# Decode attention moved out of the prompt's sixteen steps: 42 of its 128 steps go between the products of values and gate, the rest are spread over the prompt's heads

## The reference

```python
# layer 0: conv mixer, then x = x + o and the gated per-layer embedding
h = rms_norm(x, norm_g); a, b, z = split(h @ w_in, 3)
u = a * sigmoid(b); c = silu(layer_norm(depthwise_conv31(u_ext)))
o = (c * silu(z)) @ w_out
# shared keys, values and forget values, from x after layer 0
k = rms_norm(h @ kv_w[:, :1024]); v = h @ kv_w[:, 1024:2048]; logf = log_sigmoid(...)
# layer 1: forgetting attention, 16 heads of 64
q = rms_norm(h @ w_q[:, :1024]); z = h @ w_q[:, 1024:]
s = q k^T / 8 + c_q - c_k;  p = softmax(masked s);  o = p v        # c = cumsum(logf)
x = x + (o * silu(z)) @ w_out
# then the gated per-layer embedding again
```

## Time and profile before

| | |
|---|---|
| device time, median of 3 runs | 2547.67 us (2546.33 to 2551.48) |
| the profiled execution's own time | 2547.7 us |
| its span in the trace | 2546.0 us |
| TensorE busy | 2300.0 us, 90% |
| VectorE, ScalarE, GpSimd busy | 55%, 37%, 45% |
| mean granted TensorE clock | 0.958 of 2.4 GHz |
| DMA over the span | 456.25 MB, mean 179 GB/s |

### The profile page before, as it was taken

The page is one execution under the profiler, slowest core; times in us unless marked ns, Lnnn a source line. Parts: engine busy times, 40 slices in busy tenths (PEclk is TensorE's granted clock), DMA queues, the critical chain, the costliest instruction groups (busy, mean ns, idle before and its releaser), DMA issues.

```text
span 2546.0 us, 45948 instructions
## 1 busy us (share of the span) xinstructions
PE 2300.0 (90%) x15044; PEld 1862.7 (73%) x15044; DVE 1403.1 (55%) x1981; ACT 948.5 (37%) x1596; POOL 1134.8 (45%) x751
## 2 busy tenths in 40 slices
PE   5999999997458999989999996899999999899899
PEld 3999999997248998979989994445445455354499
DVE  4789988898791013166555663344443444444523
ACT  4555656665351012233102331434433344244311
POOL 0798889988563214434545544222222222220221
PEclk7999999998769999989999998999999999999999
DMA  2222222222033121025332427999999999999312
GB/s 110 71 74 68 72 80 64 72 75 70 19 107 130 45 68 42 27 92 159 121 126 103 175 94 273 383 405 383 380 397 371 341 381 381 367 372 391 147 51 81
DMA packets 142255, 456.25 MB, mean 179 GB/s; under 512 B 27441, under 2 KB 36274, under 8 KB 141170
## 3 DMA queue, kind: packets, MB, share of 16 engines
q1 hardware_dynamic: 119762, 387.73, 41.7%
q0 software_dynamic: 19712, 55.03, 6.3%
q10 hardware_dynamic: 2592, 11.14, 1.1%
HBM read 399.78 MB, written 56.13 MB: 179 GB/s over the span
## 4 chain that ended last, share of the span: by engine, by line
PE 59%; POOL 12%; issue 9%; DVE 9%; DMA 6%; ACT 4%; SPq 1%; ACTq 0%; POOLq 0%; DVEq 0%
PE PS L507 10%; PE PS L509 10%; PE PS L508 10%; POOL ACC L1239 6%; PE PS L808 4%; PE PS L787 4%; PE PS L758 4%; DMA KV<-ck 3%; PE PS L741 3%; PE PS L825 3%; PE PS L515 2%; PE PS L720 2%; POOL WL L1212 2%; DMA KV<-cv 1%; POOL ACC L1235 1%
## 5 line engine op out<-in xcount | busy, mean ns | idle before, releaser
L1212 POOL TENSOR_TENSOR WL<-RAW,WH 128x1024 fp32r<-128x1024 f32 (+1 forms) x113 | 293.2, 2595 | 393.7 <-ACT WH L879 386.7
L1570 DVE SCALAR_TENSOR_TENSOR PS<-UX,CWT,PS 128x1024 f32<-128x1024 f32 (+1 forms) x672 | 466.3, 782 | 0.0
L540 PE MATMUL PS<-HH,WH 128*128 128x384 f32 (+1 forms) x1152 | 378.5, 329 | 20.7 <-DVE HL L1556 20.7
L542 PE MATMUL PS<-HH,WL 128*128 128x384 f32 (+1 forms) x1152 | 377.4, 328 | 0.0
L541 PE MATMUL PS<-HL,WH 128*128 128x384 f32 (+1 forms) x1152 | 377.2, 327 | 0.0
L1358 POOL DMA_DIRECT2D QI<-qX_scr x128 | 76.7, 606 | 509.3 <-PE PS L720 505.7
L1239 POOL TENSOR_TENSOR ACC<-ACC,PROD 128x1088 f32<-128x1088 f32 x112 | 284.6, 2541 | 31.3 <-ACT PROD L931 25.1
L507 PE MATMUL PS<-GH,WH 128*128 128x384 f32 (+1 forms) x768 | 256.4, 334 | 16.7 <-DVE KC L1641 10.1
L509 PE MATMUL PS<-GH,WL 128*128 128x384 f32 (+1 forms) x768 | 255.4, 333 | 0.0
L508 PE MATMUL PS<-GL,WH 128*128 128x384 f32 (+1 forms) x768 | 254.2, 331 | 0.0
L540 PEld LDWEIGHTS PS<-HH,WH 128*128 128x128 f32 x1152 | 217.3, 189 | 24.7 <-issue 13.7
(11 more groups left out here) (229 smaller groups left out, 4625.3 us busy)
## 6 DMA issues: line engine op xcount, KB each, us to landing
KV<-ck SPq DMA_DIRECT2D x256, 512.0 KB, 10.5
KV<-cv SPq DMA_DIRECT2D x256, 512.0 KB, 10.8
RAW<-wA SPq DMA_DIRECT2D x48, 512.0 KB, 3.5
RAW<-wB SPq DMA_DIRECT2D x33, 512.0 KB, 3.5
QI<-qX_scr POOLq DMA_DIRECT2D x192, 64.0 KB, 5.5
RAW<-wP SPq DMA_DIRECT2D x16, 640.0 KB, 3.9
zT_scr<-ZS ACTq DMA_DIRECT2D x16, 544.0 KB, 2.7
Z<-zT_scr SPq DMA_DIRECT2D x16, 544.0 KB, 3.6
```

The lines of the kernel that those rows point to most:

```text
L540: pe.matmul(out, WH[w][:, kk], HH[:, k, a:b], start=k == 0, stop=False)
L542: mm = pe.matmul(out, WL[w][:, kk], HH[:, k, a:b], start=False, stop=k == KD - 1)
L1212: pool.tensor_tensor(WL[s][:, 0:n], RAW[s][:, 0:n], WH[s][:, 0:n].bitcast(F32), ALU.subtract).then_inc(s_lo, 1)
L1570: i = dve.scalar_tensor_tensor(out=o, in0=x, scalar=w[:, j:j + 1], in1=o, op0=ALU.mult, op1=ALU.add)
```

## The change

The decode attention gets its own step number g = 16 b + t and its own helpers (`decode_half`), and its 128 steps no longer go with the prompt's 128. A step is two halves (h = 2g and 2g + 1).

- The units come in the order forget values, keys, queries, values, gate. Steps 0 to 41 are put between the k-blocks of the last 14 of them: none in the first two value units, 2 in each of the other six, 3 in each of the first two gate units and 4 in each of the last six.
- Two steps (42, 43) come between the last unit and the first prompt step. The other 86 are spread evenly over prompt steps ("slots" x) 0 to 125: 86 of the slots have one and 42 have none.
- While the units run the pages have 2 buffers, after them 3 (before: 4, in attention only).
- On ScalarE a slot is now: copy of the decode scores, `Exp` of slot x, copy of the transposed probabilities of slot x-1, decode exponentials.
- The residual stream `X2` leaves to DRAM (`xS_scr`) after layer 0 and comes back as `X3` in attention; the first two page buffers lie where `X2` was. The past forget values are summed in the embedding phase, the new ones in the key and query units; V and gate of the prompt have two buffers each; the loops of attention are written out.
- GpSimd loads the weights of the value and gate units, since SP is then on the pages.

The core of the diff:

```diff
-U_CONV, U_OUT, U_PLE, U_K, U_V, U_F, U_Q, U_Z, U_TAIL = 0, 48, 64, 72, 80, 88, 89, 97, 105
+U_CONV, U_OUT, U_PLE, U_F, U_K, U_Q, U_V, U_Z, U_TAIL = 0, 48, 64, 72, 73, 81, 89, 97, 105
...
+        def unit_steps(u):
+
+            if u < U_V + 2:
+                return 0, 0
+            if u < U_Z:
+                return 2 * (u - U_V - 2), 2
+            m = u - U_Z
+            return (12 + 3 * m, 3) if m < 2 else (18 + 4 * (m - 2), 4)
+
+        SPOTS = {0: (), 2: (1, 3, 5, 7), 3: (1, 2, 3, 5, 6, 7), 4: tuple(range(8))}
...
+        def half_after(u, k):
+
+            g, n = unit_steps(u)
+            return 2 * g + SPOTS[n].index(k) if k in SPOTS[n] else None
...
+        G_UNITS, G_LEAD = 42, 2
+        N_SLOTS, N_STEPS = 16 * PAIRS, 16 * DB
+
+        def steps_by(x):
+
+            return min(N_STEPS + 2, G_UNITS + G_LEAD + (x + 1) * (N_STEPS + 2 - G_UNITS - G_LEAD) // (N_SLOTS - 2))
+
+        def step_of(x):
+
+            return steps_by(x - 1) if steps_by(x) > steps_by(x - 1) else None
...
+        def ring(g):
+            return g % 2 if g < G_UNITS else (g - G_UNITS) % 3
...
+            def pages(g):
+
+                b, t, s = g // 16, g % 16, ring(g)
...
+                    if kk == 0:
+                        if g == G_UNITS + 2:
+                            sp.wait_ge(s_vst, 32 * PAIRS)
+                            for x in range(2):
+                                sp.wait_ge(s_gst[x], 16 * PAIRS // 2)
+                        elif g >= G_UNITS + 3:
+                            sp.wait_ge(s_dd, g - 2)
+                        elif g >= 2:
+                            sp.wait_ge(s_dd, g - 1)
+                    sp.dma_start(KV[s][:, kk, :], at(ck if t < NG else cv, page)).then_inc(s_kv[s], 16)
...
+                if u == U_F + 2:
+                    sp.wait_ge(s_x2, KD)
+                    sp.dma_start(xS, X2[:]).then_inc(s_xs, 16)
...
+                if u == U_K + 7:
+                    sp.wait_ge(s_xs, 16)
+                    sp.wait_ge(s_gl, KD)
+                    pages(0)
+                if u == U_K + 9:
+                    pages(1)
...
+            for g in range(2, N_STEPS):
+                pages(g)
...
-                    first_unit()
+                        out = unit_bank(st, r)[:, 0:b - a]
+                        pe.matmul(out, WH[w][:, kk], GH[:, k, a:b], start=k == 0, stop=False)
+                        pe.matmul(out, WH[w][:, kk], GL[:, k, a:b], start=False, stop=False)
+                        mm = pe.matmul(out, WL[w][:, kk], GH[:, k, a:b], start=False, stop=k == KD - 1)
+                    if k == KD - 1:
+                        mm.then_inc(s_unit, 1)
+                    h = half_after(u, k)
+                    if h is not None:
+                        decode_half(h, 0)
...
+            def decode_half(h, ev):
+
+                b, t, second = h // 32, h // 2 % 16, h % 2
+                if not second:
+                    if t == 0 and b > 0:
+                        decode_pv(b - 1, NG - 1)
+                    elif b == DB:
+                        return
+                    elif 0 < t < NG:
+                        decode_scores(b, t)
+                    elif t == NG:
+                        new_transpose(b, ev)
+                    elif t > NG:
+                        decode_pv(b, t - NG - 1)
                 else:
-                    pe.wait_ge(s_kc, m)
-                    main(U_K + m, s)
-                    norm(m - 1)
-
-            def v_unit(m, s, i):
-                pe.wait_ge(s_kc, PAIRS + m)
-                main(U_V + m, s)
-                if isinstance(m, int) and m == 0:
-                    norm(PAIRS - 1)
+                    if t == 1 and b > 0:
+                        heads_transpose(b - 1, ev)
+                    elif b == DB:
+                        return
+                    elif t == 0:
+                        decode_scores(b, t)
+                    elif t == NG - 1:
+                        new_scores(b)
+                    elif t >= NG:
+                        decode_transpose(b, t - NG, ev)
...
-            pe.wait_ge(s_bcon, 1)
-            pe.wait_ge(s_pad2, 5)
-            pe.wait_ge(s_knw, 32)
-            pe.wait_ge(s_zc, PAIRS)
-            steps(pe, att_step)
+            for h in range(2 * G_UNITS, 2 * (G_UNITS + G_LEAD)):
+                decode_half(h, 0)
+            pe.wait_ge(s_zx, PAIRS)
+            h = 2 * (G_UNITS + G_LEAD) - 1
+            for x in range(N_SLOTS):
+                b, t, g = x // 16, x % 16, step_of(x)
+                scores(b, t)
+                if g is not None:
+                    h = 2 * g
+                    decode_half(h, evacs(x - 2))
+                if x > 0:
+                    prompt_transpose(x - 1, h)
+                if g is not None:
+                    h = 2 * g + 1
+                    decode_half(h, evacs(x - 1))
+                if t == 0 and b > 0:
+                    prompt_pv(b - 1, NQ - 1)
+                if b > 0:
+                    out_product(b, t)
+                if t >= 2 and t % 2 == 0:
+                    prompt_pv(b, t // 2 - 1)
+            prompt_transpose(N_SLOTS - 1, h)
+            prompt_pv(PAIRS - 1, NQ - 1)
...
-                    if started(b) or t > 0:
...
-                        atleast(act, s_pv, NQ * bb + tp // 2)
-                        for c in range((n + 511) // 512):
-                            a, e = 512 * c, min(n, 512 * c + 512)
-                            act.wait_ge(s_trp, evacs(bb, tp, c))
-                            act.activation(PT[tp % 2][:, a:e], PS[:, 5 + c, 0:e - a], ACT.Copy).then_inc(s_ev, 1)
-                    if not real:
-                        continue
-                    n = P * (item + 1)
-                    act.wait_ge(s_nm, 16 * b + t + 1)
-                    atleast(act, s_trp, evacs(b, t - 2) if started(b) or t > 1 else 0)
-                    act.activation(PP[hl][:, 0:n], PS[:, 2 * hl:2 * hl + 2, :].rearrange("p a n -> p (a n)")[:, 0:n],
...
-                    if t < NG:
...
-                        act.wait_ge(s_dd, 16 * b + t + 1)
-                        atleast(act, s_td, 9 * b)
-                        act.activation(SC[:, 512 * t:512 * t + 512], PS[:, 4, :], ACT.Copy).then_inc(s_sc, 1)
-                        continue
...
+            def scores_out(b, t):
...
+                act.wait_ge(s_dd, 16 * b + t + 1)
+                atleast(act, s_td, 9 * b)
+                act.activation(SC[:, 512 * t:512 * t + 512], PS[:, 4, :], ACT.Copy).then_inc(s_sc, 1)
...
+            def probs_out(b, t):
                 j = t - NG
                 act.wait_ge(s_td, 9 * b + j + 2)
...
                 act.activation(PTD[j % 2][:], PS[:, 6, :].rearrange("p (k n) -> p k n", n=P),
                                ACT.Copy).then_inc(s_dv, 1)
+                if j < NG - 1:
+                    dec_exp(j + 1)
...
+            silu(PAIRS - 1)
+
+
+            def prompt_exp(x):
+
+                hl = x % 2
+                n = P * (order[x % 16 // 2] + 1)
+                act.wait_ge(s_nm, x + 1)
+                atleast(act, s_trp, evacs(x - 2))
+                act.activation(PP[hl][:, 0:n], PS[:, 2 * hl:2 * hl + 2, :].rearrange("p a n -> p (a n)")[:, 0:n],
+                               ACT.Exp, bias=NMX[hl][:], accum_out=SMP[hl][:]).then_inc(s_p, 1)
+
+            def prompt_evac(x):
+
+                n = P * (order[x % 16 // 2] + 1)
+                atleast(act, s_pv, NQ * (x // 16) + x % 16 // 2)
+                for c in range((n + 511) // 512):
+                    a, e = 512 * c, min(n, 512 * c + 512)
+                    act.wait_ge(s_trp, evacs(x, c))
+                    act.activation(PT[x % 2][:, a:e], PS[:, 5 + c, 0:e - a], ACT.Copy).then_inc(s_ev, 1)
+
+            for h in range(2 * G_UNITS, 2 * (G_UNITS + G_LEAD)):
+                decode_half(h)
+            for x in range(N_SLOTS):
+                g = step_of(x)
+                if g is not None:
+                    decode_half(2 * g)
+                prompt_exp(x)
+                if x > 0:
+                    prompt_evac(x - 1)
+                if x == 3:
+                    act.wait_ge(s_unit, U_TAIL - U_OUT)
+                    act.dma_start(X3[:], xS).then_inc(s_xs, 16)
+                if g is not None:
+                    decode_half(2 * g + 1)
+            prompt_evac(N_SLOTS - 1)
```

1497 lines of the change are left out of this document (757 added, 740 removed).

## The result

The changed kernel takes 2758.12 us (median of 4 runs, 2751.49 to 2764.41) against 2549.57 us (2546.33 to 2555.20): a ratio of 1.082, 95% interval 1.079 to 1.085. It is slower, as forecast, but by 8.2% and not by 4.4%; the time lies 53 us above the range.

What follows compares the result with a forecast made beforehand. TensorE was taken to bound the kernel, with DMA just behind in attention. 2547.7 + 115 (units) - 25 (attention) + 25 (clock) = 2662.7, said as 2660 us; its own range 2610 to 2705, the overall range 2515 to 2705.

Steps and rivals of the forecast that it cites:

- gap ahead of attention: Between the last unit and the first attention slot: taken as 12 us, where the kernel before had 19.7 us.
- signs named for being wrong: Out products right behind transposes with pairs under 85 us; gate units over 27 us; first slot >20 us after last unit.
- those for being right: Gate units with four steps 22 to 25 us; last unit to attention's end 780 to 830 us; TensorE under 85% busy.
- The steps' work in the units: Units: 42 decode steps at a mean of 2.34 us lengthen TensorE's path by 98 us.
- Pages in the gate units: Six gate units with four steps: page transfers at 388 GB/s take 24.5 us against 21.6 of TensorE; +17 us.
- The upper bound: Units: +144 us if with two buffers a step waits for nearly a full landing, 8.0 us a step in 24 steps.
- the second rival: Gate units: two page buffers for 24 steps bind, a landing taking 10.5 us; whole 2689 us; chance 0.13.
- Waits in attention: Attention: TensorE waits 171 us for the copy to `PT` behind the `Exp`, plus 3 us draining after the last slot.
- Work in attention: Attention: TensorE's work of 722 us less 103 us for 44 steps moved out leaves 619 us.
- The clock: Attention: about 20 falls of TensorE's granted clock at 1.25 us each, +25 us; bounds 0 and 131 us.
- The rest, taken as nothing: Elsewhere: `X2` traffic, past sums, small copies and weight loads lie under other work; 0 us, some 5 without cover.
- TensorE stays full: Attention: VectorE and ScalarE keep ahead, waits near 5 us a pair, 679 us; whole 2512 us; chance 0.21.

Runs made afterwards that it cites:

- the run with added products: Changed kernel with ten unread small products ahead of the transposes and ten behind in each attention slot without a decode step; 2730.97 us, ratio 1.0725.
- ScalarE's order: Changed kernel with ScalarE's slot order put back: copy to `PT`, then `Exp`, then decode copies; 2660.36 us, ratio 1.045.
- both orders: Changed kernel with ScalarE's and TensorE's slot orders put back, transposes of the previous head ahead of both halves of the step; 2632.61 us, ratio 1.0335.
- the dense run with the changed kernel's orders: Changed kernel with attention's 86 steps one in each of the first 86 slots, none in the last 42; 2764.55 us, ratio 1.085.
- the counterpart with short waits: The spread run with attention's 86 steps one in each of the first 86 slots, none in the last 42; 2651.51 us, ratio 1.041.
- the spread run: Both orders, plus past forget values loaded after the embedding's input, and series and running sum split over two units each; 2624.86 us, ratio 1.030.
- TensorE's alone: Changed kernel with TensorE's slot order put back, ScalarE's `Exp` still ahead of the copy to `PT`; 2819.05 us, ratio 1.106.

## Why the prediction was right and wrong

Against the forecast sum of 2662.7 us the profiled execution is 101.7 us longer. The direction was right, and so was the chain behind the waits; the sizes of four terms were not, the clock's above all. By term: steps' work in the units -2, pages +27, gap ahead of attention +2, waits -16, work in attention +15, the clock +55, what was taken as nothing +22 and -2.

Of the signs named for being wrong one appeared (gate units over 27 us: four of the six with four steps took 29.4 to 31.2). Of those for being right two failed: gate units of 22 to 25 us, and 780 to 830 us from the last unit to the end of attention (886.7).

*The steps' work in the units, +98: right.* Two steps make a value unit 18.4 us where it was 13.85, so 2.28 us a step against 2.34. Without waits for pages the units are 568.0 us, 103.7 more than before, 7.6 of them in the two units that wait for VectorE, below; 96 are left.

*Pages in the gate units, +17: too small by 27 us.* Pages and the clock behind them cost 43.6 us (611.6 - 568.0). That the bytes of the pages bind was right; what was wrong is the rate. I put 388 GB/s, from attention's pairs; the gate units shown above ran at 306 to 333, and the fastest of the eight at 356. The upper bound was also added up wrong: at 8.0 us a step six units take 192 us, 62 more than their 130 us of work and not 46, so it should read +160 in place of +144, and the second rival 2705 in place of 2689. The measured +147 lies under that. With two buffers DMA is at times idle until one is free (share 0.85 to 0.98), while a page lands in 5.7 to 6.1 us (median), not in the 10.5 of the second rival. How much of the lower rate is due to that, and how much to the unit's own stores and loads beside the pages, was not taken apart.

*Waits in attention, 171 + 3: near, 158 us.* The chain was the right one, as the slot above and the runs on the orders show: the single wait is 2.7 us for 1024 keys. In pairs 1 to 7 TensorE idles 1.8 us in a slot without a step, as put, 1.0 us in one with a step of scores (put: 1.5) and 0.9 us in one with a step of values (put: 0.95).

*Work in attention, 619: 15 us too small.* At the full clock it is 634 us (next paragraph). The 722 us for the kernel before rest on two windows that stand some 4 us off the pairs' borders. By the first prompt scores of each pair, b=3 lasts from 1865.4 to 1971.2 us, 105.8 us with 94.4 busy, where I read 97.4 and 91.4; b=4 lasts 103.3 us, where I read 111.7. The eight pairs are busy for 750 us, 26 of them at the lower clock, so 737 at the full one; less 103 for the steps this is 634. Their idle time is 60 us, 7.5 and not 5.2 us a pair.

*The clock, +25: the step that failed, by 55 us.* "If one slot in four of the 77 without values falls, about 20 falls at 1.25 us": the number of falls was near (25 stretches at the lower clock in the attention), but they last 6.9 us on the mean and up to 17, not the length of one group of products. Together they are 172 us at 1.2 GHz, and TensorE is busy for 161 of them. At the full clock that work takes half, so the low clock costs 80 us, as the run with added products says too. This is inside the bounds of 0 and 131. I costed a fall by the longer group of products just behind the wait, and should have taken the whole stretch until the granted clock is back. Not all of it belongs to the waits for `PT`: 34 of the 172 us are in the first pair, whose clock is 0.83 here and still 0.85, 0.84 and 0.87 with ScalarE's order, both orders and the added products. Behind the first pair these runs have 0.99, 0.97 and 0.99, the changed kernel 0.91. What holds the clock down in the first pair was not tested. The Trainium skill, in "TensorE: Matmul & The Clock Gate", the section on HAM oscillation, tells of falls that come back in every round, behind waits for DMA; those waits are longer than any for `PT` here. That falls come back, the traces of the changed kernel (25 stretches) and of the last slots of the dense run with the changed kernel's orders (0.81 to 0.83) agree; the counterpart with short waits, at 0.95 to 1.00 there, hardly shows it.

*The rest, taken as nothing: +22 us, less 2 at the end.* The start of the units is 14.2 us later. ScalarE waits 8.77 us for the embedding's input; with that input loaded ahead of the past forget values, in the spread run, the units began 5.6 us earlier:

```profile
960.76 2.11 ACT L1119 ACTIVATE PH<-PR 128x1088 fp32r<-128x1088 f32 x2 [8.77 <-DMA PR<-pT]
```

And in a query unit VectorE's running sum stands ahead of the scaling that frees TensorE's banks:

```profile
1268.18 1.42 DVE L1814 TENSOR_TENSOR KC<-PS,RSTD 128x384 f32<-128x384 f32 x3 [2.22 <-PE PS L701]
...
1278.43 1.35 DVE L1826 SCALAR_TENSOR_TENSOR KN<-KC,CST,RS 128x1088 f32<-128x1088 f32 x1
1279.70 0.71 DVE L1876 TENSOR_SCALAR FL<-FL 16x1088 f32<-16x1088 f32 x1
1280.45 5.47 DVE L1879 TENSOR_TENSOR_SCAN FL<-FL,ZERO 16x1024 f32<-16x1024 f32 x9
1285.85 1.39 DVE L1814 TENSOR_TENSOR KC<-PS,RSTD 128x384 f32<-128x384 f32 x3
```

"Beside products of 12 us and more" was no cover: of a unit VectorE had 2.22 us left ahead of the scaling, and the sums take over 6 us. The other 8.6 us of the late start lie in the embedding phase, beside the past sums on VectorE (busy 87 us from 955 us to the units, 41 in the kernel before); their cause was not tested alone.

*The rivals.* "TensorE stays full" was to be decided by waits under 90 us. With both orders put back TensorE idles 81 us in attention, and the time is 2632.6, not 2512: the units still cost 141 us, and attention takes 745.6 us, not 679. Its waits are nearly twice the 45 us, its work is the 634 us, and the clock (0.95) costs some 32. "The pages bind" holds by its size, 44 us, though not by its landing time. So both the forecast and this rival happened, with a clock that was worse than in either.

## What to carry to other kernels

A step that is moved from one full stage of an engine into another costs its whole length there, and what it leaves behind may be not a shorter stage but a wait that it had covered, as here. Look, for each pair of instructions that share a buffer or bank, at what stands between them on both engines once the cover is gone, and put the short copy that is waited for ahead of the long operation that waits itself. Try the two engines' orders together and not one alone: ScalarE's alone gave 98 us here, TensorE's alone lost 61, both gave 126. Price waits on TensorE with the clock, by the whole stretch at the lower level: here the attention had 158 us of idle time and 80 us of slower products besides. Set the windows of a sum on the borders that the instructions show.

## What the runs showed of the hardware

- The changed kernel's attention and the dense run's pair without steps have the same share of idle time, 18%, and a granted clock of 0.90 and 0.98. The out product's waits for `PT` were 1.44 us a time in the first, 0.54 us in the second (mean of the last slots). So the share alone does not give the clock; that the length of the single wait does fits these two, but was not tested alone.
- Useless work can pay: 820 added products, 104 us of TensorE, made the kernel 27 us faster, as the clock rose from 0.90 to 0.98.
- DMA moved 382 to 393 GB/s at a share of 1.02 to 1.03 in full pairs with four page buffers, 384 GB/s in the dense run's first pair with three, and 306 to 356 GB/s in gate units with two.
